# Two attentions on one core: masks on VectorE instead of TensorE, key counts as logarithms, a scaling moved

## The chip, the cores and the metric

The kernel runs on one core of a Trainium2 chip. The time is the device time of one execution, in microseconds, as the median of several runs. The four compute engines (TensorE, VectorE, ScalarE, GpSimd) and the DMA queues run side by side, each through its own list of instructions, and wait for each other through semaphores.

## What is computed

Two transformer blocks follow each other on 512 tokens of width 1024. The first has differential attention (8 heads, two score maps of 64 columns each), a state space layer and a gated feed-forward part with a convolution. The second has dilated attention (8 heads of 64), a gated linear recurrence and a squared-ReLU feed-forward part. What matters here are the two softmaxes.

```python
# first block, for one block of 128 queries
s = einsum('bqhcd,bkhcd->bhcqk', qblk, k) * scale
s = where(kpos <= qpos, s, neg)
p = softmax(s)
a = p[:, :, 0] - lam * p[:, :, 1]
o = einsum('bhqk,bkhe->bqhe', a, v)
o = rmsnorm(o, subln_gain) * (1.0 - lam_init)

# second block: three branches (window, dilation) = (128, 1), (512, 4), (2048, 16),
# weighted by the softmax of their log-denominators
outs, lses = per_branch(...)
wts = softmax(stack(lses))
o = einsum('pbsh,pbshd->bshd', wts, stack(outs))
```

The weighted sum of the three branches is one softmax in which each key counts as often as it occurs in a branch: zero, one, two or three times. The kernel computes it so.

## The kernel before

Every product with weights is done in three matmuls on split operands: high part of the weight times high part and times low part of the activations, and low part of the weight times high part (`tile`, lines 580 to 582). A weight tile is 24 such matmuls of 512 columns. 216 units of weights of 512 KB stream through a ring of four buffers: SyncE loads, ScalarE makes the high part and the negated copy, a GpSimd DMA adds to make the low part. TensorE is written as one long list of tiles, with the attention's small matmuls set between them.

**First attention.** Each turn of the loop over `h` does the projections of head `h` (`k`, `q`, `v`), the scores, softmax and transposes of head `g = h - 1`, and the product with the values and the sum of squares of head `h - 2`. Queries are taken in 4 blocks `i` of 128, so block `i` has `w = 128 (i + 1)` keys. For a block and both maps `c`, `scores` (line 745 on) multiplies queries by keys into one PSUM tensor of two banks, `ps`, and adds the causal mask with a matmul of the identity by a bf16 triangle (line 754). VectorE then takes the negated maximum of both maps in one reduction (`maximum`, line 1997), ScalarE the exponential with that as bias and the sum beside it (`exps`, line 1307), VectorE combines both maps (`combine`), TensorE transposes the result (`turn`, line 762), ScalarE or VectorE copies it (`turned`, lines 1319 and 2014), and TensorE multiplies by the values (line 830). Blocks 0 and 1 of a head are done before its projection tile `q`, blocks 2 and 3 before the tile `v`. The two tensors of `ps` are used in turn by all of these steps, in an order made by `aux_order`.

The head's output gets its norm from a sum of squares on TensorE (`o_sums`) and a root on ScalarE (`head_root`, lines 1334 and 1340). VectorE scales the output by it (the step into `hid` that signals `o_done`) between its copy of the transposed block 1 and the maxima of blocks 2 and 3. All on VectorE is in program order. After the maxima come the rotation of the next head's keys, the combinations of blocks 2 and 3 and the rotation of its queries, for which the next head's scores wait (`roped`).

**Second attention.** Pairs of heads `j` take the place of heads. `scores2` adds a mask of the width of the block (line 1014). The probabilities are weighted by the count of each key in `combine2`, by a product with a running sum (`tensor_tensor_reduce` with `mult`, line 2199), which also gives the denominator; the exponential there sums nothing. The count table lies in `cst`, the masks in `msk`.

`put` on VectorE increments a semaphore and waits for it before the next instruction; `link` does so with a semaphore of VectorE's own.

Of the kernel before, what the change touches and what calls it, by code (L numbers as in the profile page):

```python
# [1 line left out]

# [5 lines left out]
P = 128  # L8
# [186 lines left out]
def build(nc, weights, x_dram, consts, rope, masks, params, ssm_b, ssm_c, lru_w, out):  # L195
    with ExitStack() as ctx:
        def sb(name, shape, dt=F32, scope=ctx):
            return scope.enter_context(nc.sbuf_tensor(name, shape, dt))
# [30 lines left out]
        with ExitStack() as first:  # L229
            gates = sb("gates", [P, 16, T], scope=first)  # L230
            with ExitStack() as s:
                mix_lo_high = sb("mix_lo_high", [P, 4, T], F32R, scope=s)
            with ExitStack() as s:
                sq_lo = sb("sq_lo", [P, 3, T], F32R, scope=s)
            y5 = sb("y5", [P, SSM_T, T], scope=first)
            with ExitStack() as s:
                gt = sb("gt", [P, 2, LANE_T, STEP + 1, GRP], scope=s)
                toep = sb("toep", [P, 2 * LANE_T, P], scope=s)
                e_sb = sb("e_sb", [P, 2, LANE_T, P], scope=s)
                lane = sb("lane", [P, 24, LANE_T], scope=s)  # L240
                pw = sb("pw", [P, 2, STEP + 1, LANE_T], scope=s)
                m16 = sb("m16", [P, GRP], scope=s)
                skip = sb("skip", [P, SSM_T, GRP], scope=s)
            with ExitStack() as s:
                rtab = sb("rtab", [P, 2, T], scope=s)
                kq_raw = sb("kq_raw", [P, 2, T], scope=s)
                kq_rs = sb("kq_rs", [P, 3, T], scope=s)
                rope_a = sb("rope_a", [P, T], scope=s)
                kq_rot = sb("kq_rot", [P, 2, T], scope=s)
                kk = sb("kk", [P, 2, T], scope=s)  # L250
                qq = sb("qq", [P, 2, T], scope=s)
                v_raw = sb("v_raw", [P, T], scope=s)
                with ExitStack() as s2:
                    g_hi = sb("g_hi", [P, SSM_T, T], F32R, scope=s2)
                    g_lo = sb("g_lo", [P, SSM_T, T], F32R, scope=s2)
                    s_hi = sb("s_hi", [P, SSM_T, T], F32R, scope=s2)
                    s_lo = g_lo
                vv = sb("vv", [P, 2, QB, P], scope=s)
                pr = sb("pr", [P, 2, 2, T], scope=s)
                pa = sb("pa", [P, 2, T], scope=s)  # L260
                pt = sb("pt", [P, QB, T], scope=s)
            o_split = sb("o_split", [P, 15, T], F32R, scope=first)
            mix_hi = sb("mix_hi", [P, KT, T], F32R, scope=first)
            mix_lo_low = sb("mix_lo_low", [P, 4, T], F32R, scope=first)
# [138 lines left out]
        ident = cst[:, C_ID:C_ID + P]  # L403
        ones = cst[:, C_ONES:C_ONES + P]
        block_ones = cst[:, C_BLK:C_BLK + P]
        mult = cst[:, C_MULT:C_MULT + T]
        ident_b = msk[:, M_ID:M_ID + P]

        def par(name, i=0):
            a, w = PARAMS[name]  # L410
# [152 lines left out]
        def _(pe):  # L563
# [183 lines left out]
            def scores(h, i):  # L747
                bank, w = s_use(("s", h, i)), P * (i + 1)
                pe.wait_ge(roped, 2 * h + 2)
                for c in range(2):  # L750
                    r = slice(64 * c, 64 * c + 64)
                    pe.matmul(bank[:, c, 0:w], qq[r, h % 2, P * i:P * i + P], kk[r, h % 2, 0:w], start=True, stop=False)  # L752
                for c in range(2):
                    last = pe.matmul(bank[:, c, P * i:w], ident_b, msk[:, M_TRI:M_TRI + P], start=False, stop=True)  # L754
                last.then_inc(ps_full, 1)

            def turn(h, i):
# [250 lines left out]
            def scores2(j, i):  # L1008
                bank, w = s_use(("p", j, i)), P * (i + 1)
                for c in range(2):  # L1010
                    r = slice(64 * c, 64 * c + 64)
                    pe.matmul(bank[:, c, 0:w], qq2[r, j % 2, P * i:P * i + P], kk2[r, j % 2, 0:w], start=True, stop=False)  # L1012
                for c in range(2):
                    last = pe.matmul(bank[:, c, 0:w], ident_b, msk[:, M_UNI + T - w:M_UNI + T], start=False, stop=True)  # L1014
                last.then_inc(ps_full, 1)

            def turn2(j, i):
# [110 lines left out]
        def _(act):  # L1128
# [169 lines left out]
                put(act.activation(g_hi[:, t], y5[:, t], ACT.Copy), xhi_done)  # L1298

            act.dma_start(rtab[:], rope).then_inc(r_landed, 16)  # L1300
            def exps(use, dst, w, i, negmax, sums):

                act.wait_ge(maxed, EXPS[use] + 1)
                bank = ps_ready(act, use)
                for c in range(2):
                    kw = {"accum_out": sums[:, i % 2, 2 + c:3 + c]} if sums is not None else {}
                    ins = act.activation(dst[:, c, 0:w], bank[:, c, 0:w], ACT.Exp, bias=negmax[:, i % 2, c:c + 1], **kw)  # L1307
                    ins.then_inc(ps_free[SUSE[use] % 2] if c else act_c, 1)

            def exps1(h, i):  # L1310
                if 4 * h + i >= 2:
                    act.wait_ge(combed, 4 * h + i - 1)
                exps(("s", h, i), pr[:, i % 2], P * (i + 1), i, soft, soft)

            def turned(h, i):

# [190 lines left out]
            def exps2(j, i):  # L1507
                n = 4 * j + i
                if n >= 2:

                    ps_ready(act, ("t2", (n - 2) // 4, (n - 2) % 4))
                exps(("p", j, i), pr2[:, i % 2], P * (i + 1), i, soft2, None)

            def values2(j):

# [172 lines left out]
        def _(dve):  # L1688
            sent = {}

            def put(ins, s):

                ins.then_inc(s, 1)
                sent[s.name] = sent.get(s.name, 0) + 1
                dve.wait_ge(s, sent[s.name])
# [298 lines left out]
            def maximum(use, w, i, s):  # L1994

                bank = ps_ready(dve, use)
                put(dve.tensor_reduce(s[:, i % 2, 0:2], bank[:, :, 0:w], AX.X, ALU.max, negate=True), maxed)  # L1997

            def combine(h, i):

# [29 lines left out]
            def o_rest(h):  # L2030
                py_read(dve, ("pv", h))
                sums_rest(h, 2, hid[:, h])

            def rope_step(h, name, n, ready, dst):
                evacuated(dve, (name, h))
                stt(rope_a[:], kq_raw[:, n], par(("kg", "qg")[n]), rtab[:, 0])
                dve.wait_ge(swapped[n], 64 * (h + 1))
                link(stt(kq_rot[:, n], kq_rot[:, n], gain_swapped[:, n:n + 1], rtab[:, 1]))
                link(tt_(rope_a[:], rope_a[:], kq_rot[:, n], ALU.add))
                dve.wait_ge(ready, h + 1)  # L2040
                put(tt_(dst[:, h % 2], rope_a[:], kq_rs[:, n]), roped)

            def ssm_out(n):
                for m in (2 * n, 2 * n + 1):
                    free(tt_(mix(m), done(("ssm", m)), gates[:, 8 + m]), ("ssm", m))

            kq_rest(0, "k", 0)
            dve.wait_ge(r_landed, 16)
            ts(rtab[0:32, 1], rtab[0:32, 1], -1.0, ALU.mult)
# [8 lines left out]
            for h in range(1, HEADS + 2):  # L2058
# [11 lines left out]
                    combine(g, 1)  # L2070
                if 2 <= h <= HEADS:
                    o_rest(h - 2)
                if attends:
                    turned(g, 1)
                if h < HEADS:
# [4 lines left out]
                if h == HEADS + 1:  # L2080
                    for o in (5, 6):
                        o_low(o)
                if h >= 2:
                    py_read(dve, ("pv", h - 2))
                    dve.wait_ge(rs_o, h - 1)
                    put(stt(hid[:, h - 2], hid[:, h - 2], lam_t[:, 6:7], kq_rs[:, 2]), o_done)
                if attends:
                    maximum(("s", g, 2), 3 * P, 2, soft)
                    maximum(("s", g, 3), 4 * P, 3, soft)
# [10 lines left out]

            o_low(HEADS - 1)
            for m in range(KT + 1):
                if m < KT:
                    if m in GATES_LAST:
                        dve.wait_ge(gate_done, m - GATES_LAST[0] + 1)
                    free(tt_(nrm[:, m % 2], done(("attn", m)), gates[:, m]), ("attn", m))
                    evacuated(dve, ("attn", m))
                    put(tt_(mix(m), mix(m), nrm[:, m % 2], ALU.add), src_done)
                if m > 0:
                    split_lo(SPLIT["mix"] + m - 1, mix_lo(m - 1), mix(m - 1), mix_hi[:, m - 1])  # L2110
# [83 lines left out]
            def combine2(j, i):  # L2194

                w, s = P * (i + 1), soft2[:, i % 2]
                ps_read(dve, ("p", j, i))
                for c in range(2):
                    link(dve.tensor_tensor_reduce(pr2[:, i % 2, c, 0:w], pr2[:, i % 2, c, 0:w], mult[:, T - w:T], 1.0, 0.0,
                                                  ALU.mult, ALU.add, s[:, 2 + c:3 + c]))  # L2200
                link(dve.reciprocal(s[:, 4:6], s[:, 2:4]))
                ts(pr2[:, i % 2, 0, 0:w], pr2[:, i % 2, 0, 0:w], s[:, 4:5], ALU.mult)
                put(ts(pr2[:, i % 2, 1, 0:w], pr2[:, i % 2, 1, 0:w], s[:, 5:6], ALU.mult), combed)
# [271 lines left out]
```

## Time and profile before

| | us |
|---|---|
| median of 3 runs | 1413.63 (1412.9 to 1413.95) |
| profiled execution | 1414.0 |
| its span, first to last instruction | 1411.8 |
| TensorE matmul busy | 1389.5 (98%) |
| TensorE weight load busy | 1122.1 (79%) |
| ScalarE busy | 834.1 (59%) |
| VectorE busy | 691.2 (49%) |
| GpSimd busy | 202.6 (14%) |

The first attention lies at 183 to 390 us, the second at 885 to 1000 us. The granted clock of TensorE is 0.997 of full speed. A busy time is the sum of the instructions' records. Records of matmuls overlap, so for TensorE the distances between starts say more than the lengths. An idle time in brackets behind an instruction names what ended the engine's wait before it.

### The profile page before, as it was taken

What the parts mean: (1) busy time and instruction counts of PE and PEld (TensorE: products, weight loads), DVE (VectorE), ACT (ScalarE), POOL (GpSimd) and SP (SyncE); (2) the same over time, 40 slices, a digit from 0 to 9 for tenths busy, and PEclk for the clock granted to TensorE, in tenths of its full rate; (3) what the DMA queues carried; (4) which work ended last, traced back from release to release, by engine and by line L of the source; (5) the groups of instructions that cost most, each with busy time, mean ns of one, the idle gap of its engine ahead of it and who ended that gap; (6) DMA issues with size and microseconds to landing.
All of it is one profiled execution on the core that took longest, in us unless ns stands there. A gap on an engine that the chain in (4) does not pass through costs nothing.

```text
span 1411.8 us, 18495 instructions
## 1 busy us (share of the span) xinstructions
PE 1389.5 (98%) x6770; PEld 1122.1 (79%) x6770; DVE 691.2 (49%) x1234; ACT 834.1 (59%) x1181; POOL 202.6 (14%) x236
## 2 busy tenths in 40 slices
PE   7999999999999999999999999999999999999998
PEld 4888877777778888888888887777797888888887
DVE  6993477877633455544154164746354301213324
ACT  7556666777755656665365476654666655535442
POOL 1111100100111111111111111110111111111111
PEclk9999999999999999999999999999999999999999
DMA  9996976565579888888978996755676898898873
GB/s 289 212 190 173 223 169 142 135 159 140 122 196 228 187 188 197 186 197 196 215 167 195 216 228 162 169 130 118 136 173 156 188 218 185 193 201 180 206 165 89
DMA packets 82692, 254.76 MB, mean 180 GB/s; under 512 B 16816, under 2 KB 20016, under 8 KB 82608
## 3 DMA queue, kind: packets, MB, share of 16 engines
q0 software_dynamic: 32400, 117.98, 46.1%
q1 hardware_dynamic: 48768, 132.50, 31.7%
q10 hardware_dynamic: 1440, 3.15, 0.6%
q8 instruction: 54, 0.88, 0.3%
q14 instruction: 30, 0.25, 0.1%
HBM read 128.03 MB, written 3.41 MB: 93 GB/s over the span
## 4 chain that ended last, share of the span: by engine, by line
PE 93%; DVE 3%; ACT 2%; DMA 1%; issue 1%; DVEq 0%; ACTq 0%
PE pg L580 26%; PE pg L582 26%; PE pg L581 26%; PE ps L752 2%; PE py L830 1%; DMA w_lo<-w_raw 1%; PE ps L1012 1%; PE ps L1022 1%; PE ps L762 1%; DVE pairs L1710 1%; PE py L1032 1%; DVE acc L1713 1%; PE ps L754 0%; PE ps L1014 0%; PE px L653 0%
## 5 line engine op out<-in xcount | busy, mean ns | idle before, releaser
L580 PE MATMUL pg<-x_hi,w_hi 128*128 128x512 f32 x1072 | 423.6, 395 | 3.4 <-ACT rel L1655 2.4
L582 PE MATMUL pg<-x_hi,w_lo 128*128 128x512 f32 x1072 | 418.3, 390 | 0.0
L581 PE MATMUL pg<-x_lo,w_hi 128*128 128x512 f32 x1072 | 417.9, 390 | 0.0
L544 POOL DMA_DIRECT2D w_lo<-w_raw x221 | 191.0, 864 | 1163.2 <-ACT w_lo L1146 1091.7
L1145 ACT ACTIVATE w_hi<-w_raw 128x1024 fp32r<-128x1024 f32 x216 | 227.1, 1051 | 103.6 <-PE pg L582 99.7
L580 PEld LDWEIGHTS pg<-x_hi,w_hi 128*128 128x128 f32 x1072 | 201.6, 188 | 46.9 <-DMA w_lo<-w_raw 4.2
L582 PEld LDWEIGHTS pg<-x_hi,w_lo 128*128 128x128 f32 x1072 | 201.6, 188 | 42.6
L581 PEld LDWEIGHTS pg<-x_lo,w_hi 128*128 128x128 f32 x1072 | 201.8, 188 | 41.9 <-issue 1.0
L1146 ACT ACTIVATE w_lo<-w_raw 128x1024 fp32r<-128x1024 f32 x216 | 225.9, 1046 | 0.0
L580 PE MATMUL pg<-act_hi,w_hi 128*128 128x512 f32 x424 | 164.9, 389 | 0.0
L581 PE MATMUL pg<-act_lo,w_hi 128*128 128x512 f32 x424 | 164.9, 389 | 0.0
L582 PE MATMUL pg<-act_hi,w_lo 128*128 128x512 f32 x424 | 164.9, 389 | 0.0
L582 PEld LDWEIGHTS pg<-act_hi,w_lo 128*128 128x128 f32 x424 | 79.6, 188 | 16.5
L580 PEld LDWEIGHTS pg<-act_hi,w_hi 128*128 128x128 f32 x424 | 79.6, 188 | 16.5
L581 PEld LDWEIGHTS pg<-act_lo,w_hi 128*128 128x128 f32 x424 | 79.6, 188 | 16.5
L1710 DVE TENSOR_TENSOR cu<-pg,rstd 128x512 f32<-128x512 f32 x44 | 30.4, 692 | 114.6 <-PE pg L582 114.6
L1710 DVE TENSOR_TENSOR pairs<-rel 128x512 f32<-128x512 f32 x32 | 22.2, 692 | 129.0 <-ACT rel L1655 123.3
L1710 DVE TENSOR_TENSOR hid<-hid,pg 128x512 f32<-128x512 f32 x32 | 22.0, 687 | 103.0 <-PE pg L582 98.9
L1713 DVE SCALAR_TENSOR_TENSOR cnv<-cu,prm,cnv 128x511 f32<-128x511 f32 x88 | 66.1, 751 | 3.1
L1710 DVE TENSOR_TENSOR acc<-acc,pg 128x512 f32<-128x512 f32 (+1 forms) x24 | 16.2, 677 | 92.0 <-PE pg L582 91.3
L1997 DVE TENSOR_REDUCE soft<-ps 128x2 f32<-128x256 f32 (+3 forms) x48 | 39.6, 825 | 13.8 <-PE ps L754 8.6
L1307 ACT ACTIVATE pr<-ps,soft 128x128 f32<-128x128 f32 (+3 forms) x64 | 33.3, 529 | 16.9 <-DVE soft L1997 15.3
(431 smaller groups left out, 1816.1 us busy)
## 6 DMA issues: line engine op xcount, KB each, us to landing
w_raw<-weights SPq DMA_DIRECT2D x226, 512.0 KB, 4.7
w_lo<-w_raw POOLq DMA_DIRECT2D x221, 512.0 KB, 5.7
kq_rot<-kq_raw SPq DMA_DIRECT2D x64, 64.0 KB, 2.9
hid<-x SPq DMA_DIRECT2D x4, 512.0 KB, 5.6
hid<-x ACTq DMA_DIRECT2D x8, 256.0 KB, 5.5
act_lo<-w_raw POOLq DMA_DIRECT2D x4, 512.0 KB, 6.9
out<-hid SPq DMA_DIRECT2D x16, 128.0 KB, 1.8
u_dram<-hid SPq DMA_DIRECT2D x4, 256.0 KB, 5.4
```

What stands on the lines that cost most here:

```text
L544: pool.dma_start(low_of(u), w_raw[:, s], accum_op=ALU.add).then_inc(lo_in[s], 16)
L580: pe.matmul(bank[:], wh, xh(k), start=n == 0, stop=False)
L581: pe.matmul(bank[:], wh, xl(k), start=False, stop=False)
L582: last = pe.matmul(bank[:], wl, xh(k), start=False, stop=n == len(ks) - 1)
L752: pe.matmul(bank[:, c, 0:w], qq[r, h % 2, P * i:P * i + P], kk[r, h % 2, 0:w], start=True, stop=False)
L762: last = pe.transpose(bank[:, 0, P * j:P * j + P], pa[:, i % 2, P * j:P * j + P], ident)
L1145: act.activation(high_of(u), w_raw[:, s], ACT.Copy)
L1146: put(act.activation(low_of(u), w_raw[:, s], ACT.Copy, scale=-1.0), hi_done)
L1307: ins = act.activation(dst[:, c, 0:w], bank[:, c, 0:w], ACT.Exp, bias=negmax[:, i % 2, c:c + 1], **kw)
L1710: return dve.tensor_tensor(out_, a, b, op)
L1713: return dve.scalar_tensor_tensor(out_, a, s, b, op0, op1)
L1997: put(dve.tensor_reduce(s[:, i % 2, 0:2], bank[:, :, 0:w], AX.X, ALU.max, negate=True), maxed)
```

## The change

The mask matmuls are taken out of both score steps. VectorE's `maximum` becomes two instructions per block, one for each map: it adds the mask to the scores, multiplies by -1, writes the result back to PSUM and keeps the minimum, which is the negated maximum. ScalarE takes the exponential with a scale of -1 and sums in both attentions. In the first attention the mask is a table `tri` of zeros with the triangle at its end. In the second the table of counts is turned once into the logarithm of the count plus the mask (`logarithms`, three instructions among the attention projection tiles), so the two weighting passes of `combine2` go. The scaling of a head's output moves to the next turn of the loop, behind the squares of the head after it (`o_scale`); the last two heads keep the old place.

```diff
@@ scores
-                    pe.matmul(bank[:, c, 0:w], qq[r, h % 2, P * i:P * i + P], kk[r, h % 2, 0:w], start=True, stop=False)
-                for c in range(2):
-                    last = pe.matmul(bank[:, c, P * i:w], ident_b, msk[:, M_TRI:M_TRI + P], start=False, stop=True)
+                    last = pe.matmul(bank[:, c, 0:w], qq[r, h % 2, P * i:P * i + P], kk[r, h % 2, 0:w], start=True, stop=True)
                 last.then_inc(ps_full, 1)
@@ scores2
-                    pe.matmul(bank[:, c, 0:w], qq2[r, j % 2, P * i:P * i + P], kk2[r, j % 2, 0:w], start=True, stop=False)
-                for c in range(2):
-                    last = pe.matmul(bank[:, c, 0:w], ident_b, msk[:, M_UNI + T - w:M_UNI + T], start=False, stop=True)
+                    last = pe.matmul(bank[:, c, 0:w], qq2[r, j % 2, P * i:P * i + P], kk2[r, j % 2, 0:w], start=True, stop=True)
@@ exps (ScalarE)
-                    kw = {"accum_out": sums[:, i % 2, 2 + c:3 + c]} if sums is not None else {}
-                    ins = act.activation(dst[:, c, 0:w], bank[:, c, 0:w], ACT.Exp, bias=negmax[:, i % 2, c:c + 1], **kw)
+                    ins = act.activation(dst[:, c, 0:w], bank[:, c, 0:w], ACT.Exp, bias=s[:, i % 2, c:c + 1], scale=-1.0,
+                                         accum_out=s[:, i % 2, 2 + c:3 + c])
@@ maximum (VectorE)
-                put(dve.tensor_reduce(s[:, i % 2, 0:2], bank[:, :, 0:w], AX.X, ALU.max, negate=True), maxed)
+                mask = tri[:, T - w:T] if use[0] == "s" else multi[:, T - w:T]
+                for c in range(2):
+                    last = dve.tensor_tensor_reduce(bank[:, c, 0:w], bank[:, c, 0:w], mask, -1.0, 3.0e38, ALU.add, ALU.min,
+                                                    s[:, i % 2, c:c + 1])
+                put(last, maxed)
@@ new on VectorE
+            def o_scale(h):
+                py_read(dve, ("pv", h))
+                dve.wait_ge(rs_o, h + 1)
+                put(stt(hid[:, h], hid[:, h], lam_t[:, 6:7], kq_rs[:, 2]), o_done)
+            def logarithms():
+                c, t = multi, rstd[:]
+                bend = math.log(3) / 2 - math.log(2)
+                link(ts(t, c, bend, ALU.mult, math.log(2) - 2 * bend, ALU.add))
+                link(stt(c, c, -1.0, t, ALU.add, ALU.mult))
+                link(tt_(c, c, msk[:, M_UNI:M_UNI + T], ALU.add))
+            dve.memset(tri[:, 0:T - P], 0.0)
+            link(dve.tensor_copy(tri[:, T - P:T], msk[:, M_TRI:M_TRI + P]))
             kq_rest(0, "k", 0)
@@ loop over h (VectorE)
                 if 2 <= h <= HEADS:
                     o_rest(h - 2)
+                if 3 <= h <= HEADS:
+                    o_scale(h - 3)
                 if attends:
                     turned(g, 1)
...
-                if h >= 2:
-                    py_read(dve, ("pv", h - 2))
-                    dve.wait_ge(rs_o, h - 1)
-                    put(stt(hid[:, h - 2], hid[:, h - 2], lam_t[:, 6:7], kq_rs[:, 2]), o_done)
+                if h >= HEADS:
+                    o_scale(h - 2)
@@ attention projection tiles
             for m in range(KT + 1):
+                if m == 3:
+                    logarithms()
@@ combine2
-                for c in range(2):
-                    link(dve.tensor_tensor_reduce(pr2[:, i % 2, c, 0:w], pr2[:, i % 2, c, 0:w], mult[:, T - w:T], 1.0, 0.0,
-                                                  ALU.mult, ALU.add, s[:, 2 + c:3 + c]))
                 link(dve.reciprocal(s[:, 4:6], s[:, 2:4]))
```

## Rows read from the trace of the kernel before

**Rows 1.** The page: busy time by engine; the chain that ended last, by engine.
```profile
PE 1389.5 (98%) x6770; PEld 1122.1 (79%) x6770; DVE 691.2 (49%) x1234; ACT 834.1 (59%) x1181; POOL 202.6 (14%) x236
...
PE 93%; DVE 3%; ACT 2%; DMA 1%; issue 1%; DVEq 0%; ACTq 0%
```

**Rows 2.** Timeline of TensorE, first attention: start, length in us, line, operation.
```profile
233.39 0.28 PE L754 MATMUL ps<-msk 128*128 128x128 bf16 x2
233.51 2.38 PE L830 MATMUL py<-pt,vv 128*128 128x512 f32 x8
...
243.41 0.28 PE L754 MATMUL ps<-msk 128*128 128x128 bf16 x2
243.63 1.13 PE L752 MATMUL ps<-kk,qq 64*128 64x512 f32 x4
244.69 0.28 PE L754 MATMUL ps<-msk 128*128 128x128 bf16 x2
244.79 0.47 PE L580 MATMUL pg<-x_hi,w_hi 128*128 128x512 f32 x1
```

**Rows 3.** Timeline of TensorE, second attention.
```profile
896.23 0.63 PE L1022 MATMUL ps<-cst,prob 128*128 128x128 f32 x4 [0.70 <-DVE prob L1716]
...
954.26 0.39 PE L1014 MATMUL ps<-msk 128*128 128x256 bf16 x2
954.40 0.47 PE L580 MATMUL pg<-x_hi,w_hi 128*128 128x512 f32 x1
954.72 0.39 PE L581 MATMUL pg<-x_lo,w_hi 128*128 128x512 f32 x1
954.95 0.40 PE L582 MATMUL pg<-x_hi,w_lo 128*128 128x512 f32 x1
...
961.68 0.50 PE L1014 MATMUL ps<-msk 128*128 128x384 bf16 x2
962.11 1.13 PE L1012 MATMUL ps<-kk,qq 64*128 64x512 f32 x4
963.17 0.60 PE L1014 MATMUL ps<-msk 128*128 128x512 bf16 x2
963.43 0.58 PE L580 MATMUL pg<-x_hi,w_hi 128*128 128x512 f32 x1
963.85 0.40 PE L581 MATMUL pg<-x_lo,w_hi 128*128 128x512 f32 x1
```

**Rows 4.** Timeline of TensorE, value transposes and first scores, second and fourth head.
```profile
206.05 0.60 PE L820 MATMUL px<-cst,v_raw 128*128 128x128 f32 x4
206.58 0.49 PE L752 MATMUL ps<-kk,qq 64*128 64x128 f32 x4
...
257.01 0.60 PE L820 MATMUL px<-cst,v_raw 128*128 128x128 f32 x4
257.68 0.49 PE L752 MATMUL ps<-kk,qq 64*128 64x128 f32 x4
```

**Rows 5.** Timeline of VectorE, one head and an attention projection tile.
```profile
241.82 0.42 DVE L2014 COPY pt<-ps 128x256 f32<-128x256 f32 x1 [1.92 <-PE ps L762]
...
245.40 0.75 DVE L1713 SCALAR_TENSOR_TENSOR hid<-hid,lam_t,kq_rs 128x512 f32<-128x512 f32 x1 [1.09 <-ACT kq_rs L1340]
...
256.84 0.69 DVE L1710 TENSOR_TENSOR qq<-rope_a,kq_rs 128x512 f32<-128x512 f32 x1
...
416.37 0.69 DVE L1710 TENSOR_TENSOR pairs<-pg,gates 128x512 f32<-128x512 f32 x1 [3.25 <-PE pg L582]
```

**Rows 6.** Lines 1997, 2199 and 1680: durations in ns, min/median/max.
```profile
L1997 DVE TENSOR_REDUCE soft<-ps x48: 424/824/1226, 184.6 to 985.6; 128x2 f32<-128x256 f32 x12, 128x2 f32<-128x512 f32 x12, 128x2 f32<-128x768 f32 x12, 128x2 f32<-128x1024 f32 x12
...
L2199 DVE CUSTOM_DVE_ANT_0 prob<-prob,cst x32: 291/492/694, 893.0 to 989.8; 128x128 f32<-128x128 f32 x8, 128x256 f32<-128x256 f32 x8, 128x384 f32<-128x384 f32 x8, 128x512 f32<-128x512 f32 x8
L2199 DVE DVE_READ_ACCUMULATOR2_ANT soft<- x32: 80/82/85, 893.2 to 990.4; 128x1 f32 x32
...
L1680 ACT ACTIVATE px<-rstd x1: 389/389/389, 1397.5 to 1397.5; 128x256 f32<-128x256 f32 x1
```

More of the change, by code:

```diff
@@ L1 @@
+import math
 from contextlib import ExitStack
@@ L234, in build @@
                 sq_lo = sb("sq_lo", [P, 3, T], F32R, scope=s)
+                tri = sb("tri", [P, T], BF16, scope=s)
             y5 = sb("y5", [P, SSM_T, T], scope=first)
@@ L405, in build @@
         block_ones = cst[:, C_BLK:C_BLK + P]
-        mult = cst[:, C_MULT:C_MULT + T]
-        ident_b = msk[:, M_ID:M_ID + P]
+        multi = cst[:, C_MULT:C_MULT + T]
         def par(name, i=0):
@@ L1300, in _, with exps @@
             act.dma_start(rtab[:], rope).then_inc(r_landed, 16)
-            def exps(use, dst, w, i, negmax, sums):
+            def exps(use, dst, w, i, s):
                 act.wait_ge(maxed, EXPS[use] + 1)
@@ L1312, in exps1 @@
                     act.wait_ge(combed, 4 * h + i - 1)
-                exps(("s", h, i), pr[:, i % 2], P * (i + 1), i, soft, soft)
+                exps(("s", h, i), pr[:, i % 2], P * (i + 1), i, soft)
             def turned(h, i):
@@ L1511, in exps2 @@
                     ps_ready(act, ("t2", (n - 2) // 4, (n - 2) % 4))
-                exps(("p", j, i), pr2[:, i % 2], P * (i + 1), i, soft2, None)
+                exps(("p", j, i), pr2[:, i % 2], P * (i + 1), i, soft2)
             def values2(j):
```

## The prediction

> **What bounds the kernel now.** I read the busy shares first, then the chain that ended last, then what TensorE waited for, and last the order of time around the score blocks. TensorE is busy for 98% of the span and makes up 93% of the chain, VectorE is busy for 49% of it and makes up 3% of the chain [rows 1]. Matmul records overlap, so 98% is not by itself a proof; what counts is how the starts follow each other. In a weight tile the starts of two matmuls of 512 columns lie 954.95 - 954.72 = 0.23 us apart, one behind the other without a hole [rows 3]. So an instruction that leaves TensorE's queue gives its start-to-start time back, not the length of its record (the masks' records are 0.28 us long for a pair and overlap what follows), and an instruction that VectorE or ScalarE gains costs nothing as long as its result still comes before TensorE asks for it. The questions are therefore: what do the masks cost between starts, where does VectorE come late today, and does it come late elsewhere after the change.
>
> **Masks in the first attention.** There are 8 heads of 4 score blocks, each with a pair of bf16 mask matmuls (128 columns each), 32 pairs. What a pair costs depends on what stands behind it [rows 2]. Behind it is another score block (blocks 0 and 2): 243.63 - 243.41 = 0.22 us. Behind it is the product with the values (block 1): 233.51 - 233.39 = 0.12. Behind it is a weight tile (block 3): 244.79 - 244.69 = 0.10. Per head 0.22 + 0.12 + 0.22 + 0.10 = 0.66, less a rounding of 0.01 each that the other heads show, so 0.65; times 8 is **5.2 us**. What is not in the trace is a score block with a weight tile right behind it. The switch can cost less than now, since the first matmul behind the masks takes 954.72 - 954.40 = 0.32 us to the next start where 0.23 is usual [rows 3], or it can cost up to 0.1 us more than now, if the weight load that the masks cover comes into the open. With a tenth more or less at two switches of each head the term lies between 3.6 and 6.8. I take the rows as they stand.
>
> **Masks in the second attention.** 4 pairs of heads with 4 blocks, and here the masks are as wide as the block [rows 3]. Block 0 (128 columns) is the same instruction as above, 0.22. Block 1 (256 columns, a tile behind it): 954.40 - 954.26 = 0.14. Block 2 (384): 962.11 - 961.68 = 0.43. Block 3 (512): 963.43 - 963.17 = 0.26, and the tile's first matmul then needs 963.85 - 963.43 = 0.42 to the next start instead of 0.32, so 0.10 more is the masks' own. Sum 1.15 per pair of heads, times 4 is **4.6 us**, with the same doubt at the switches 3.8 to 5.4.
>
> The Trainium skill, VectorE: DVE Perf Modes, section "The TRN2 errata", gives a matmul max(60, 6 + columns) cycles at 2.4 GHz. By it 64 masks of 128 columns are an estimated 3.6 us and the 32 of the second attention an estimated 4.3 us, 7.9 where rows 2 and 3 give 9.8; the rows hold what the page leaves out, the switch between score block and mask.
>
> **A stall that the moved scaling removes.** TensorE transposes the values of a head (4 short transposes) and then begins the scores. In the second head the scores start 206.58 - 206.05 = 0.53 us behind the transposes, in the fourth 257.68 - 257.01 = 0.67 [rows 4]. The difference, 0.12 to 0.14, is a wait: the rotated queries are finished on VectorE at 256.84 + 0.69 = 257.53, and a semaphore's way of 0.15 later the scores begin [rows 4, 5]. The six heads from the third on show it, so 6 x 0.125 = **0.75 us**. This is a loop, and it says that VectorE's second half of a head is just too long today. In that half it holds 1.09 us of idleness in front of the scaling of the head output, which waits for ScalarE's root, then the scaling of 0.75 [rows 5]. All that follows, the maxima of blocks 2 and 3, both rotations and two combinations, is queued behind this wait. The change puts the scaling of the head before into the first half, where its root is long there and where VectorE idles 1.92 us in front of its copy [rows 5].
>
> **VectorE's new maxima.** A reduction of both halves of a block takes 0.424 us for 2 x 128 elements and 1.226 for 2 x 512 [rows 6], so 1.04 ns per element and about 0.16 fixed. In its place come two passes with an accumulator each. The nearest row is the very operation in the second attention, on SBUF: 0.291 us for 128 and 0.694 for 512 elements [rows 6]. With the accumulator's read of 0.08 each, which partly overlaps, two passes are 0.67 us for 128 (0.42 before) and about 1.5 for 512 (1.23 before): 0.25 to 0.33 more per block, some 1.2 us per head. That source and result are in PSUM is new. A source in PSUM costs nothing more here: a product that reads a tile's bank takes 0.69 us for 512 elements, as one on SBUF does [rows 5]. Of a VectorE result in PSUM the trace has no row; ScalarE's in PSUM takes 0.389 us for 256 elements [rows 6], which is no more than its other short passes. I take the SBUF price, and as the upper bound twice the time per element. The lower bound is the reduction's own price, which would leave all else as it is.
>
> Is it covered? A head lasts (257.68 - 206.58) / 2 = 25.55 us [rows 4]. First half: the maxima of blocks 0 and 1 add 0.6, the scaling comes in with 0.75, and TensorE arrives 0.34 earlier (two pairs of masks), in all 1.7 against 1.92 of idleness, so the copy is hardly late, and the score block that waits for it starts over 1 us after it. Second half: 1.09 + 0.75 + 0.04 leave, 0.65 comes in, TensorE arrives 0.32 earlier, and 0.12 is missing today, so 1.88 - 0.65 - 0.32 - 0.12 = **0.8 us of slack** remain. That frees ScalarE's exponentials of blocks 2 and 3 by 1.2 us too.
>
> **The second attention's other side.** Its combination loses two weighting passes per block (16 blocks), its maxima gain 0.25 to 0.33 per block. For blocks 0 and 1 that is 2 x 0.33 + 2 x 0.47 = 1.6 less and 0.6 more, 1.0 us earlier. TensorE's one wait for a combination there, 0.70 us at 896.23 [rows 3], asks for just this, and goes: **0.7 us**. Its other waits there are for copies and stay. ScalarE gains 32 reads of an accumulator, under 0.25 us each, on an engine that is busy 59% [rows 1] and ahead of the combinations by more than that; nothing.
>
> **At nothing.** The memset and the copy of the triangle (two short passes, under 0.6 us) stand ahead of the first head's key squares, which TensorE sums only behind two ssm units, 48 matmuls or 11 us at 0.23. The three passes of the logarithms (2.1 us at 0.69 to 0.75) stand in the 3.25 us that VectorE idles for each attention projection tile [rows 5]. Without that cover the two would cost 2.7 us together. The negative scale of the exponential is a field of the same instruction.
>
> **Sum.** 5.2 + 4.6 + 0.75 + 0.7 = 11.25 us. The profiled execution took 1414.0 us for a span of 1411.8; it becomes 1402.75. It stands 0.4 above the median of 1413.63, which becomes **1402.4 us**. A change within 0.2% (2.8 us) counts as none.
>
> **The rivals.**
> **Only the masks go.** VectorE's relief is eaten, because the maximum of block 3 has to wait for block 3 itself and the reading of the sums takes longer than I think. Then 9.8 remain, 1403.8. For it: the wait removed is short (0.12). Against it: the slack of 0.8 is more than six times as much. Chance 0.14; it lies in my range.
> **A dear result in PSUM.** At two cycles per element the maxima of blocks 2 and 3 take 2 x 896 x 1.04 ns = 1.87 us more in the second half of each head, 1.07 over the slack. Seven heads hand on to a next one: 7.5 lost, and the 0.75 as well; 11.25 - 8.25 = 3.0 remain, 1410.6. In the second attention 0.8 more per half stays under the 1.0 that leaves. For it: no row; against it: the PSUM rows above. Chance 0.08.
> **Slower: VectorE becomes the bound.** The same place, from the point at which the second half of a head grows by 0.8 + 10.5 / 7 = 2.3 us, that is at 2.3 us / 1792 elements = 1.3 ns more per element than 1.04. At three times the time per element (reading, writing back and accumulating one after the other) it grows by 3.7, so 2.9 over the slack; 7 heads lose 20.3, the gain of 10.5 stands against it, and the second attention loses at most 1 per pair of heads, its first blocks growing by 1.6 where 1.0 has left: 14 us, 1427. For it: both sides of the operation use one memory. Against it: the same operation on SBUF runs at the speed of a plain addition, 0.694 and 0.69 us [rows 5, 6]. Chance 0.04.
>
> **How the numbers follow.** Forecast 0.74, the rivals 0.14, 0.08 and 0.04. The bounds of the terms give 3.6 + 3.8 = 7.4 us at the least and 6.8 + 5.4 + 0.75 + 0.7 = 13.65 at the most, 1406.2 to 1400.0. I widen it to 1399.5 to 1407, since the terms are of starts that the profile models, which leaves out the two last rivals, 0.12. Faster: 0.74 + 0.14 and 0.05 of the third case, which lies close to the border, 0.93; no change 0.03; slower 0.04.
>
> **What would show it.** A score block followed by the next start after its own time alone (1.06 us for block 3 [rows 2]); starts of the scores 0.53 behind the transposes in all heads; a head of 24.8 us; two maximum passes of 0.29 to 0.69 us each; VectorE idle behind its first half's copy but no longer in front of the scaling; no wait at the first combination of the second attention. I am wrong if the passes last over 1 us for 512 elements, if TensorE's waits name the rotated queries or a combination, or if score blocks grow by what the masks covered.

## The result

The changed kernel takes 1402.53 us (median of 4 runs, 1401.73 to 1403.03) against 1413.79 for the kernel before on the same chip, 11.3 us less: a ratio of 0.9918 with a 95% interval of 0.9906 to 0.9930. A second series gave 1402.24 against 1414.27, a ratio of 0.9908 (0.9894 to 0.9921). The forecast was 1402.4 with a range of 1399.5 to 1407.0, so time and sign are right; below stands which of its terms are right and which only add up.

The page after the change, busy time by engine and the chain by engine (answers to [rows 1]):

```profile
PE 1377.8 (98%) x6674; PEld 1116.7 (80%) x6674; DVE 685.5 (49%) x1319; ACT 835.7 (60%) x1213; POOL 201.9 (14%) x236
...
PE 92%; DVE 4%; ACT 2%; DMA 1%; issue 1%; DVEq 0%; ACTq 0%
```

Shares alone say nothing here: they are the same as before. TensorE has 96 matmuls less, VectorE 85 instructions more and 5.7 us less of work: the weighting passes of the second attention took 15.7 us, while the 96 new passes (45.6 us) take 6.0 more than the reductions they replace (39.6), and the reads of the accumulators lie in good part beside a pass.

What the masks left behind shows in the order of time. TensorE after the change, first attention (start, length, line, operation), to be held against [rows 2, 4]:

```profile
228.37 0.60 PE L819 MATMUL px<-cst,v_raw 128*128 128x128 f32 x4
228.90 1.19 PE L753 MATMUL ps<-kk,qq 64*128 64x128 f32 x8
...
230.01 2.42 PE L829 MATMUL py<-pt,vv 128*128 128x512 f32 x8
...
239.11 1.34 PE L753 MATMUL ps<-kk,qq 64*128 64x384 f32 x6
...
240.81 0.50 PE L581 MATMUL pg<-x_hi,w_hi 128*128 128x512 f32 x1
241.15 0.40 PE L582 MATMUL pg<-x_lo,w_hi 128*128 128x512 f32 x1
...
253.07 0.60 PE L819 MATMUL px<-cst,v_raw 128*128 128x128 f32 x4
253.60 1.19 PE L753 MATMUL ps<-kk,qq 64*128 64x128 f32 x8
```

The scores now start 0.53 us behind the value transposes in the fourth head too (253.60 - 253.07), the stall of [rows 4] is gone, and a head lasts 253.07 - 228.37 = 24.70 us (its period) instead of 25.55. The same stretches before:

```profile
232.12 0.49 PE L752 MATMUL ps<-kk,qq 64*128 64x128 f32 x4
...
242.57 0.92 PE L752 MATMUL ps<-kk,qq 64*128 64x384 f32 x4
```

Blocks 0 and 1 took 233.51 - 232.12 = 1.39 us and now take 230.01 - 228.90 = 1.11, so 0.28 less where 0.34 was forecast. Blocks 2 and 3 took 244.79 - 242.57 = 2.22 and now take 240.81 - 239.11 = 1.70, 0.52 less where 0.32 was forecast: without a mask between them the score matmuls of the two blocks themselves stand closer (1.90 of their own before, 1.70 now). The first tile matmul behind them costs 0.34, as it did within 0.03.

Blocks 0 and 1 keep a wait that no matmul row names, because matmul records overlap. It stands at the weight load (PEld) of block 1's scores. VectorE's copy, this weight load, and the total of such waits in the changed kernel (us, times, longest):

```profile
228.64 0.69 DVE L2015 COPY pt<-ps 128x512 f32<-128x512 f32 x1 [0.76 <-PE ps L761]
...
229.38 0.30 PEld L753 LDWEIGHTS ps<-kk,qq 64*128 64x128 f32 x4 [0.18 <-DVE pt L2015]
...
PEld ps L753 <- DVE pt L2015: 1.3, 7, 0.2
```

By `aux_order` block 1's scores are written into the tensor of `ps` that this copy of the transposed block 3 empties, and they start 229.38 - 228.64 - 0.69 = 0.05 us behind its end. From the second head on they start 0.49 us behind block 0's, and in the first head, with no such copy ahead, 0.33. The kernel before has no wait of this kind: with block 0's masks between them the distance was 0.64. So these masks give back 0.15 us in seven heads and 0.31 in the first, and some 0.16 us per head, 1.1 in all, are still spent waiting. No run moves the copy; this is read from the traces alone.

The new maxima, line 1996, on VectorE (durations in ns, min/median/max):

```profile
L1996 DVE DVE_READ_ACCUMULATOR2_ANT soft<- x96: 138/141/144, 183.2 to 974.5; 128x1 f32 x96
L1996 DVE CUSTOM_DVE_ANT_0 ps<-ps,tri x64: 298/516/733, 183.0 to 367.3; 128x128 f32<-128x128 f32 x16, 128x256 f32<-128x256 f32 x16, 128x384 f32<-128x384 f32 x16, 128x512 f32<-128x512 f32 x16
```

Source and result in PSUM cost 298 to 733 ns, where the same operation on SBUF took 291 to 694 [rows 6]. The means of 315 and 715 ns for 128 and 512 elements give 1.04 ns per element, as for the reduction, so neither a double nor a triple time per element exists. VectorE in the fourth head:

```profile
236.57 0.75 DVE L1710 SCALAR_TENSOR_TENSOR hid<-hid,lam_t,kq_rs 128x512 f32<-128x512 f32 x1
238.36 0.42 DVE L2015 COPY pt<-ps 128x256 f32<-128x256 f32 x1 [1.04 <-PE ps L761]
...
240.88 0.56 DVE L1996 CUSTOM_DVE_ANT_0 ps<-ps,tri 128x384 f32<-128x384 f32 x1
241.36 0.14 DVE L1996 DVE_READ_ACCUMULATOR2_ANT soft<- 128x1 f32 x1
241.36 0.60 DVE L1996 CUSTOM_DVE_ANT_0 ps<-ps,tri 128x384 f32<-128x384 f32 x1
...
243.49 0.75 DVE L1710 SCALAR_TENSOR_TENSOR rope_a<-kq_raw,prm,rtab 128x512 f32<-128x512 f32 x1
...
251.88 0.69 DVE L1707 TENSOR_TENSOR qq<-rope_a,kq_rs 128x512 f32<-128x512 f32 x1
```

The scaling (236.57) stands ahead of the copy and waits for nothing, and 1.04 us of idleness are left in front of the copy. The read of one accumulator runs beside the next pass (both at 241.36), so the four passes of blocks 2 and 3 take 243.49 - 240.88 = 2.61 us. The two reductions in the kernel before took 248.44 - 246.19 = 2.25:

```profile
246.19 2.22 DVE L1997 TENSOR_REDUCE soft<-ps 128x2 f32<-128x768 f32 x2
248.44 0.75 DVE L1713 SCALAR_TENSOR_TENSOR rope_a<-kq_raw,prm,rtab 128x512 f32<-128x512 f32 x1
```

After the change the rotated queries are ready at 251.88 + 0.69 + 0.15 = 252.72, and the scores start at 253.60: **0.88 us of slack**, the forecast had 0.8. This is the slack in front of block 0. The copy that block 1's scores wait for comes right behind the rotated queries on VectorE, and there VectorE is ahead by less, the 0.76 us of idleness in the copy's row above.

### The profile page after: what moved, and what is told of

It is laid out like the page before. It is cut to its first block, busy times and chain, and to the rows that moved or that the text cites. A ratio compares the mean times of both kernels' runs of the same rounds, so it can differ in the third digit from the quotient of the medians.

```text
span 1400.8 us, 18420 instructions
## 1 busy us (share of the span) xinstructions
PE 1377.8 (98%) x6674; PEld 1116.7 (80%) x6674; DVE 685.5 (49%) x1319; ACT 835.7 (60%) x1213; POOL 201.9 (14%) x236
## 4 chain that ended last, share of the span: by engine, by line
PE 92%; DVE 4%; ACT 2%; DMA 1%; issue 1%; DVEq 0%; ACTq 0%
PE pg L581 27%; PE pg L582 27%; PE pg L583 27%; PE ps L753 2%; PE py L829 1%; PE ps L1011 1%; PE ps L761 1%; PE ps L1019 1%; DMA act_lo<-w_raw 1%; DMA w_lo<-w_raw 1%; DVE pairs L1707 1%; PE py L1029 1%; DVE acc L1710 1%; PE px L654 0%; DVE acc L1707 0%
## 5 line engine op out<-in xcount | busy, mean ns | idle before, releaser
L1176 ACT ACTIVATE act_hi<-pairs 128x512 fp32r<-128x512 f32 x32 | 20.2, 632 | 33.3 <-DVE pairs L1707 33.3
```

The source lines that it names most:

```text
L1176: put(act.activation(dst, src, ACT.Copy), xhi_done)
```

## Where the time went, stage by stage

Each stage is a distance between two starts on TensorE: the first attention from the first head's value transposes to the first attention projection, the second from its first value transposes to the first tile of its output projection. Before and after:

```profile
183.28 0.60 PE L820 MATMUL px<-cst,v_raw 128*128 128x128 f32 x4
...
387.11 0.48 PE L580 MATMUL pg<-o_split,w_hi 128*128 128x512 f32 x1
...
887.65 0.60 PE L1043 MATMUL px<-cst,v_raw 128*128 128x128 f32 x4
...
995.90 0.50 PE L580 MATMUL pg<-mx_hi,w_hi 128*128 128x512 f32 x1
```

```profile
181.83 0.60 PE L819 MATMUL px<-cst,v_raw 128*128 128x128 f32 x4
...
378.93 0.48 PE L581 MATMUL pg<-o_split,w_hi 128*128 128x512 f32 x1
...
880.60 0.60 PE L1040 MATMUL px<-cst,v_raw 128*128 128x128 f32 x4
...
983.04 0.50 PE L581 MATMUL pg<-mx_hi,w_hi 128*128 128x512 f32 x1
```

The same four starts were read in every kernel's trace. In the second and third traces of the unaltered kernels both stages came out the same within 0.03 us, which makes them sharper than the median of a whole run. Over different kernels the second attention is less sharp: with the same code in it it takes 102.14 to 102.44 us, and the long ones have a wait of 0.24 that the others lack.

| kernel | first attention | between | second attention | time (median) |
|---|---|---|---|---|
| before | 203.83 | 500.54 | 108.25 | 1413.79 |
| before, second trace | 203.80 | 501.63 | 108.24 | 1414.8 (one run) |
| only the scaling moved | 203.08 | 502.00 | 108.23 | 1412.92 |
| changed, scaling in its old place | 203.79 | 500.64 | 102.44 | 1408.86 |
| no masks at all | 201.57 | 500.53 | 104.69 | 1408.54 |
| no masks, scaling moved | 197.10 | 501.71 | 104.58 | 1403.43 |
| first attention changed | 197.06 | 500.53 | 108.23 | 1406.27 |
| second attention changed | 203.77 | 500.50 | 102.23 | 1406.69 |
| changed | 197.10 | 501.67 | 102.44 | 1402.53 |
| changed, second trace | 197.10 | 501.88 | 102.44 | 1402.24 |
| changed, third trace | 197.11 | 500.50 | 102.44 | 1400.77 (one run) |
| changed, one needless product per head | 197.50 | 500.61 | 102.23 | 1400.63 |
| the same again | 197.50 | 500.53 | 102.14 | 1401.88 |
| changed, three needless products per head | 209.36 | 501.85 | 102.19 | 1414.36 |

So the change takes 6.73 us out of the first attention and 5.81 out of the second, 12.5 in all. Between the stages the same tiles run in every kernel, and their time varies by 1.5 us from trace to trace, up and down.

## The experiments

**The scaling moved, and nothing else.** The edit is the one of the diff, in the kernel before.

```diff
                     o_rest(h - 2)
+                if 3 <= h <= HEADS:
+                    o_scale(h - 3)
...
-                if h >= 2:
-                    py_read(dve, ("pv", h - 2))
-                    dve.wait_ge(rs_o, h - 1)
-                    put(stt(hid[:, h - 2], hid[:, h - 2], lam_t[:, 6:7], kq_rs[:, 2]), o_done)
+                if h >= HEADS:
+                    o_scale(h - 2)
```

> The kernel before with only the scaling of the head output moved to the next turn of the loop. Masks, maxima and weighting stay as before. Theory (the stall of 0.12 us in front of the scores of six heads comes from VectorE's second half of a head): the scores start 0.53 us behind the value transposes in all heads, the time falls by 0.75 us to about 1413.0. Rival (the distance of 0.65 is no wait for VectorE): it stays 0.65 and the time stays at 1413.8.

```profile
257.23 0.60 PE L820 MATMUL px<-cst,v_raw 128*128 128x128 f32 x4
257.76 0.49 PE L752 MATMUL ps<-kk,qq 64*128 64x128 f32 x4
```

That is TensorE in the fourth head of this kernel: 0.53 us, where the kernel before shows 0.67 [rows 4]. The first attention is 203.83 - 203.08 = 0.75 us shorter, to the hundredth what was forecast. The whole time is 1412.92 against 1413.95, a ratio of 0.9995 (0.9986 to 1.0004), which by itself can't be told from none; the stage shows it.

**The changed kernel with the scaling in its old place.**

```diff
                 if 2 <= h <= HEADS:
                     o_rest(h - 2)
-                if 3 <= h <= HEADS:
-                    o_scale(h - 3)
...
-                if h >= HEADS:
+                if h >= 2:
                     o_scale(h - 2)
```

> The changed kernel with the scaling put back to its old place. Theory: the period of a head is a loop through TensorE (scores of block 0 to transposes of block 1) and VectorE (copy of block 1 to rotated queries). It was 25.55 us; the masks of blocks 0 and 1 take 0.28 from TensorE's part, the maxima of blocks 2 and 3 add 0.36 to VectorE's, so 25.63 against 24.70 in the changed kernel: 7 x 0.93 = 6.5 us, about 1409. Rival (the moved scaling is worth only the stall that could be seen before, 0.75 us): 1403.3.

It takes 1408.86 us (ratio 0.9962, 0.9948 to 0.9975). TensorE's waits (total, times, longest), those of its weight loads, and the fourth head:

```profile
PE ps L753 <- DVE qq L1707: 5.4, 6, 0.9
...
PEld ps L753 <- DVE pt L2015: 2.2, 7, 0.3
```

```profile
254.66 0.60 PE L819 MATMUL px<-cst,v_raw 128*128 128x128 f32 x4
256.16 1.34 PE L753 MATMUL ps<-kk,qq 64*128 64x128 f32 x8 [0.90 <-DVE qq L1707]
```

The first attention is as long as before the change (203.79 against 203.83): **all that the masks free there is lost again in waits for VectorE**, for the rotated queries and for the copy behind them. Moved alone the scaling is worth 0.75 us, moved together with the masks 203.79 - 197.10 = 6.69. The wait is 1.50 - 0.53 = 0.97, as forecast for the period (0.93); the period itself is 25.82 and not 25.63. The score blocks behind the wait take 1.27 us instead of 1.11 (their merged record is 1.34 long, not 1.19), because the copy now runs right behind the rotated queries and block 1's scores wait longer for it, 0.33 us at their weight load instead of 0.18. Six heads pay this, not the seven of the expectation, so its time of 1409 is met with both errors against each other.

**No masks at all**, first with the scaling in its old place and then with it moved.

```diff
-                    pe.matmul(bank[:, c, 0:w], qq[r, ...], kk[r, ...], start=True, stop=False)
-                for c in range(2):
-                    last = pe.matmul(bank[:, c, P * i:w], ident_b, msk[:, M_TRI:M_TRI + P], start=False, stop=True)
+                    last = pe.matmul(bank[:, c, 0:w], qq[r, ...], kk[r, ...], start=True, stop=True)
...
+                if m == 3:
+                    link(dve.memset(mult, 1.0))
```

> The kernel before without the mask matmuls and with nothing in their place: neither attention is masked, and the table of key counts is set to one. VectorE's maxima, weighting and scaling are as before. Theory: the loop through VectorE holds the first attention at 25.55 - 0.28 = 25.27 us per head, so it keeps 7 x 0.57 = 4.0 us of what TensorE gave up; the last head and the second attention gain in full. 1402.5 + 4.0 + 0.7 (the wait for the first combination of the second attention stays) = 1407.2. Rival (a matmul removed is time gained): 1413.8 - 9.8 = 1404.0 or less.

> The same without masks (neither attention is masked, key counts are one), and with the scaling moved. Theory: TensorE's list is that of the changed kernel and the first attention is bound by it, so VectorE's dearer maxima cost the changed kernel nothing: head period 24.70, only the wait of 0.7 for the first combination of the second attention differs, 1403.2. Rival (the two passes per block lie on the path): faster than the changed kernel by up to 8 x 0.7 = 5.6 us, 1397.

They take 1408.54 (0.9964, 0.9950 to 0.9977) and 1403.43 us (0.9928, 0.9914 to 0.9941). TensorE's waits in the first of them:

```profile
PE ps L752 <- DVE qq L1706: 3.2, 6, 0.5
...
PE ps L1018 <- DVE prob L1712: 2.1, 3, 1.2
```

In the first attention the kernel without masks gains 2.3 us (203.83 - 201.57), and with the scaling moved it is exactly as fast as the changed kernel (197.10 both), 6.7 us shorter than before. So the 64 extra passes on VectorE cost nothing there: the rival by which they lie on the path is out. In the second attention the two differ: 104.6 against 102.44 us. Here the masks' removal brings TensorE to the combinations earlier than VectorE is, and the wait grows from 0.70 [rows 3] to 2.1 us. Dropping the weighting passes takes this away, 2.2 us in all, not the 0.7 that the kernel before showed. I had expected 1407.2 and 1403.2. Missing in the first were 0.15 us in each of six heads, in which block 1's scores wait for the copy, and in both this larger wait. By its stages the second kernel should take 1402.5 + 2.1 = 1404.6, and its traced run took 1404.85; that its median lies so close to 1403.2 is luck.

**Each attention alone.** The edits are the changed kernel with one attention's lines set back to the old ones; for the first alone:

```diff
+                if use[0] != "s":
+                    put(dve.tensor_reduce(s[:, i % 2, 0:2], bank[:, :, 0:w], AX.X, ALU.max, negate=True), maxed)
+                    return
                 mask = tri[:, T - w:T] if use[0] == "s" else multi[:, T - w:T]
```

with the masks of `scores2`, the plain exponential and the weighting of `combine2` restored and the logarithms left out, and the mirror image of it for the second, with the scaling in its old place.

> The change in the first attention alone: masks, maxima, negative scale and moved scaling there; the second attention as before. Theory: from the two traces the first attention is 6.7 us shorter in the changed kernel, so about 1407.1. Rival (what the trace says of starts is modelled and the first attention gives only what its masks' 64 short matmuls take at full rate, 3.6 us, with 0.75): 1409.4.

> The change in the second attention alone: masks, maxima, logarithms, sums on ScalarE there; the first attention as before, its scaling in the old place. Theory: the second attention is 5.8 us shorter by the traces, so about 1408.0; with the first attention's 6.7 the two make 12.5, more than the 11.3 measured for both. The rest is waits for weights that fall at other places, so the two gains may add up to between 11 and 13. Rival (the second attention gives the masks' matmuls at full rate alone, 4.3 us): 1409.5.

They take 1406.27 (0.9950, 0.9936 to 0.9963) and 1406.69 us (0.9951, 0.9937 to 0.9964). By stage the gains are 6.77 and 6.02, and neither alters the other's stage. By the medians they are 7.4 and 7.0, 14.4 together, which is more than the 11.3 to 12.0 of the whole change. The stages say 12.8 for the two and 12.5 for the whole. As no stage holds the rest, it lies in the stretches that no edit touches; only the traced run of each series can be split like this.

**Needless products on VectorE**, to measure the slack: one, then three, behind the maxima of blocks 2 and 3.

```diff
                     maximum(("s", g, 3), 4 * P, 3, soft)
+                    for _ in range(1 if h < HEADS else 0):
+                        link(tt_(rope_a[:], kq_raw[:, 0], kq_raw[:, 0]))
```

> The changed kernel with one needless VectorE product of 512 elements (0.73 us) behind the maxima of blocks 2 and 3 in each of the first seven heads. Theory: the changed kernel's rotated queries are ready 0.9 us before TensorE asks for them (251.88 + 0.69 + 0.15 = 252.72 against scores at 253.60), so nothing changes: 1402.5 to 1402.8. Rival (the loop through VectorE still sets the pace, as in the kernel before): 7 x 0.73 = 5.1 us more, 1407.6.

> The same with three such products (2.19 us). Theory: 2.19 - 0.88 = 1.31 us over the slack, seven times: 9.2 us more, 1411.7, and the scores start 0.53 + 1.31 us behind the value transposes. Rival (other slack hides more, since ScalarE and the next copy also move): under 1408.

One product of 0.73 us fits: the period stays 24.70, and only the second head, where the slack is smaller, waits, 0.28 us before block 0 and 0.15 at block 1 (first attention 0.4 us longer). Three don't. The fourth head, and the granted clock of TensorE just after it (start and end of the stretch, its length, busy time by engine, then the clock, DMA share and GB/s):

```profile
256.34 0.60 PE L819 MATMUL px<-cst,v_raw 128*128 128x128 f32 x4
258.17 1.34 PE L753 MATMUL ps<-kk,qq 64*128 64x128 f32 x8 [1.23 <-DVE qq L1707]
...
260.00:263.00 3.00, 3.00 (x6) 1.60 (x5) 2.79 (x10) 1.32 (x6) 0.00 (x0) 0.50 0.67 150
```

258.17 - 256.34 = 1.83 is 0.53 + 1.30, so the slack before block 0 is 2.19 - 1.30 = 0.89 us, as read. The time misses the forecast, though: 1414.36 (1.0005, 0.9994 to 1.0017) instead of 1411.7. The stage is 12.3 us longer and not 9.2. Six heads pay 1.45 each and not 1.31, since block 1's scores wait 0.15 longer for the copy. What a head can hide is thus 2.19 - 1.45 = 0.74 us, about the 0.76 of idleness before the copy. The second head pays 1.9.

The rest, 1.7 us, is the clock. In the fourth head the product with the values takes 3.87 us instead of 2.18, and TensorE's granted clock there is 0.50, the lower of its two levels, where the stages of the other traces show 1.00. Before it fell, TensorE had waited 1.23 us ahead of the scores, as it does in the later heads too, in which the clock stays. The eleven runs of this kernel have mean granted clocks of 0.993 to 0.997, the kernel before beside them 0.996 to 0.998; the two slowest (1418.12 and 1417.67) have 0.994 and 0.993, the fastest (1410.11) 0.997. So a good part of the miss in the median goes with the clock and not with VectorE's work. That TensorE's waits bring the lower clock on is not shown.

**The unaltered kernels once more**, since one needless product had seemed to make the kernel faster (1400.63 against 1402.53 in another series).

> The changed kernel once more, unaltered, beside the next run on the same chip. Question: do the waits for weights (0.8 us at 819 us and 1.4 us for the fourth unit of the last feed-forward part in its first trace) come back in a second trace? If they belong to the phase in which this kernel meets its transfers, they do, and it takes 1402.5. If they are drawn anew in each execution, they lie elsewhere or are missing, and the median is the same while the trace is not.

> The kernel with one needless product per head once more, unaltered, on the same chip as the changed kernel. It took 1400.6 where the changed kernel had taken 1402.5 in another session. If the phase of the transfers is what differs, it is 1.5 to 2 us faster again. If the sessions differ and not the kernels, both take the same within 0.5 us.

> The kernel before once more, for a second trace. Its first trace had one wait of 1.0 us for a weight, at 107 us. If such waits come from the phase, it is there again.

> The changed kernel, for a third trace; expectations as for the second. The attention stages must be 197.1 and 102.4 us long in all three traces, and only the waits for weights may differ.

Side by side they take 1402.24 and 1401.88 us, the same. TensorE's waits for weights in the changed kernel's first trace:

```profile
PE ps L887 <- DMA act_lo<-w_raw: 1.4, 1, 1.4
...
PE pg L581 <- DMA w_lo<-w_raw: 0.8, 1, 0.8
```

in its third:

```profile
PE pg L581 <- DMA w_lo<-w_raw: 1.3, 1, 1.3
...
PE ps L887 <- DMA act_lo<-w_raw: 0.7, 1, 0.7
```

and in the second trace of the kernel before, which had shown one wait of 1.0 at first:

```profile
PE pg L580 <- DMA w_lo<-w_raw: 2.6, 3, 0.9
...
PE ps L888 <- DMA act_lo<-w_raw: 0.4, 1, 0.4
```

The waits for weights are other ones in each execution, 0.2 to 3.1 us in sum over all the traces, in both kernels. They belong to neither kernel. A second source lies beside them, behind the second attention (same columns as above), in the first and the third trace of the changed kernel:

```profile
1068.00:1074.00 6.00, 6.00 (x20) 4.74 (x20) 2.95 (x5) 4.69 (x8) 1.19 (x2) 0.72 0.74 173
...
1068.00:1074.00 6.00, 4.67 (x21) 3.55 (x20) 2.77 (x4) 5.17 (x8) 0.86 (x1) 1.00 1.00 219
```

The granted clock is 0.72 in the first and 1.00 in the third, whose waits for weights sum to nearly the same (2.0 against 2.2 us), though it is 2.3 us faster (1400.77 against 1403.03). A difference of 1 or 2 us between two traces or two series is put down to these waits and this clock until a stage shows it.

## Why the prediction was right, point by point

- **Masks by distance of starts.** Right in kind, somewhat low in size. The first attention without its stall gives 6.73 - 0.75 = 6.0 us where 5.2 stood, within the bounds of 3.6 and 6.8. The part that is over is the blocks 2 and 3: the two score blocks overlap more when no mask lies between them (0.52 instead of 0.32 per head). Blocks 0 and 1 stay under the forecast (0.28 instead of 0.34), since VectorE's copy holds block 1 back.
- **The second attention's masks and its wait**, 4.6 + 0.7 = 5.3, measured 5.81. TensorE after the change:

```profile
942.71 0.93 PE L1011 MATMUL ps<-kk,qq 64*128 64x128 f32 x8
943.57 0.50 PE L581 MATMUL pg<-x_hi,w_hi 128*128 128x512 f32 x1
...
950.01 2.01 PE L1011 MATMUL ps<-kk,qq 64*128 64x384 f32 x8
951.95 0.53 PE L581 MATMUL pg<-x_hi,w_hi 128*128 128x512 f32 x1
```

  Blocks 0 and 1 take 0.86 us and blocks 2 and 3 1.94, and before, from the same starts:

```profile
952.98 0.49 PE L1012 MATMUL ps<-kk,qq 64*128 64x128 f32 x4
...
960.84 0.92 PE L1012 MATMUL ps<-kk,qq 64*128 64x384 f32 x4
```

  954.40 - 952.98 = 1.42 and 963.43 - 960.84 = 2.59. That is 0.56 + 0.65 = 1.21 less, and about 0.08 at the first matmul of the tile behind block 3 (0.06 in this pair), some 1.29 per pair of heads where 1.15 stood. Four times 1.29 and the wait of 0.70 are 5.9. A small new wait takes some of it back: 0.24 us once for the copy of block 1.
- **The Trainium skill's figure for a matmul** (VectorE: DVE Perf Modes, section "The TRN2 errata"). The estimate of 7.9 us by its cycle count is too low for all masks: the stages, less the stall of 0.75 and the wait of 0.7, give 11.1. The count leaves out the switch between score block and mask, and here the measurement decides. What in the switch takes the time is not shown.
- **The stall and the moved scaling.** The 0.75 us are right to the hundredth. But the prediction booked the move at that price, and its other half, that without the move the masks bring nothing in the first attention, stands only between the lines of its slack: 0.12 missing, and TensorE arriving earlier.
- **VectorE's passes.** Mis-sized upwards. 0.65 us was put in for blocks 2 and 3 and 0.6 for blocks 0 and 1. Measured are 0.36 and nearly nothing, since the accumulator's read runs beside the next pass and the first maxima wait for their scores anyway. In the slack this gave 0.29, while TensorE arrives 0.52 us earlier and not 0.32: 1.88 - 0.36 - 0.52 - 0.12 = 0.88. The idleness before the copy is 1.04 instead of 0.2. Both cost nothing, as they were hidden either way.
- **A path that the sum left out.** The prediction asked whether the copy of block 1 holds up a score block. It did not ask this of the copy of block 3, which comes behind the rotated queries and for which block 1's scores wait. That costs the changed kernel some 0.16 us in seven heads, and it makes the slack 0.76 and not 0.88. The sum came out all the same, because the masks of blocks 2 and 3 gave more than was booked.
- **Rivals.** "Only the masks go" fell: the stall is gone in all heads. "A dear result in PSUM" and "VectorE becomes the bound" fell with the durations of line 1996. The mechanism of the third is real, and its price was shown by the three needless products: 2.19 us more in the second half of a head make the kernel as slow as it was before, 1.7 us of this trace being the lower clock.
- **The sum.** By stage 12.5 us, not 11.25; the medians give 11.3 and 12.0. In the traced pair the start (183.28 - 181.83) is 1.45 us shorter too, but the stretch between the attentions is 1.13 longer and the one behind them 1.86 (1400.8 - 983.04 against 1411.8 - 995.90), which leaves 11.0; 1.2 of that are more waits for weights (2.2 against 1.0). That the first median lies within 0.1 us of the forecast is luck; the forecast is right within about 1 us.

## What to carry to other kernels

A visible stall prices an edit only while everything else stays. Where two engines take turns in a loop, ask who is ahead and by how much: here 0.12 us of stall meant that of a gain of 6 us on TensorE only 2.3 would stay with VectorE's work as it was, and nothing with the longer maxima, unless VectorE's path got shorter too. Two edits worth 0.75 and nothing by themselves gave 6.7 together. Look at the waits of the weight loads as well as those of the matmuls. Price a removed matmul by the distance between starts, and compare stages between fixed starts rather than medians when transfers add noise of their own.

## What was not expected of the hardware

- A wait of TensorE can stand in the rows of its weight loads alone: 0.18 us in each of seven heads of the changed kernel, of which 0.16 reach the starts of the matmuls (0.49 instead of 0.33 us from block 0 to block 1), while no matmul row names it.
- A VectorE pass that reads and writes PSUM costs up to 6% more than on SBUF (733 against 694 ns at 512 elements), the longest being those that start together with the read of an accumulator. This read is longer, 141 ns against 82, but the first of each pair lies beside the next pass.
- Score matmuls of two blocks in a row stand 0.2 us closer than with a bf16 mask between them (1.70 against 1.90 us for blocks 2 and 3).
- A granted clock of 0.50 over some 3 us made one product with the values 3.87 us long instead of 2.18, in the middle of a TensorE stage.
